# Gathers of an expert layer issued in blocks of eight U rows and eight V rows instead of one U and one V in turn

## What is computed

```
def expert_block(args):
    ht, it, gt = args                    # 128 tokens, their 128 indices, their 128 gates
    ue = jnp.take(u, it, axis=0)
    act = jax.nn.gelu(jnp.einsum('tkd,td->tk', ue, ht), approximate=False)
    ve = jnp.take(v, it, axis=0)
    return jnp.einsum('tk,tkd->td', gt * act, ve)
```

## Time and profile before

| What | us |
|---|---|
| median of three runs | 1722.1 |
| the profiled execution | 1728.55 |
| its span | 1727.2 |
| first gather starts | 974.32 |
| last gather starts | 1711.45 |
| from there to the end of the span | 15.75 |

### The profile page before, as it was taken

The page is one execution under the profiler, slowest core; times in us unless marked ns, Lnnn a source line. Parts: engine busy times, 40 slices in busy tenths (PEclk is TensorE's granted clock), DMA queues, the critical chain, the costliest instruction groups (busy, mean ns, idle before and its releaser), DMA issues.

```text
span 1727.2 us, 19148 instructions
## 1 busy us (share of the span) xinstructions
PE 1498.9 (87%) x7183; PEld 1085.7 (63%) x7183; DVE 1079.7 (63%) x1970; ACT 660.7 (38%) x1102; POOL 547.4 (32%) x608
## 2 busy tenths in 40 slices
PE   7999999998999899999999888997775764867775
PEld 6888897887798788888899764543222321323222
DVE  5766645687654666665657576657745755756644
ACT  5545534785453554553735221312211221211111
POOL 1000001211000000000100356666666766766664
PEclk9999999999999999999999999999997987989888
DMA  8555454333353455574444889999999999999997
GB/s 282 179 187 195 150 183 157 107 134 125 106 189 121 156 190 180 193 193 137 130 138 159 292 299 372 346 370 365 370 381 364 362 370 363 388 366 377 369 377 277
DMA packets 199942, 431.87 MB, mean 250 GB/s; under 512 B 20773, under 2 KB 114090, under 8 KB 199850
## 3 DMA queue, kind: packets, MB, share of 16 engines
q0 software_dynamic: 73728, 268.47, 40.8%
q1 hardware_dynamic: 123312, 159.66, 28.5%
q10 hardware_dynamic: 2810, 2.52, 0.5%
HBM read 429.55 MB, written 1.05 MB: 249 GB/s over the span
## 4 chain that ended last, share of the span: by engine, by line
PE 56%; POOL 12%; issue 11%; DVE 10%; ACT 6%; another core or an unknown queue 3%; DMA 2%; DVEq 1%; ACTq 0%; POOLq 0%
PE ps L431 56%; POOL GS L2701 6%; POOL RAW L2701 4%; DVE WL L1789 3%; ACT WH L1261 2%; POOL AR L2701 1%; DMA RAW<-in_peer_v_dram,AR 1%; DMA RAW<-in_peer_u_dram,AR 1%; DVE XN L1826 1%; DVE GS L2538 1%; POOL LB L2701 1%; DVE H L1831 0%; DVE AR L2054 0%; DVE XX L1845 0%
## 5 line engine op out<-in xcount | busy, mean ns | idle before, releaser
L431 PE MATMUL ps<-XX,WH 128*128 128x256 f32 (+1 forms) x1872 | 467.4, 330 | 10.0 <-DVE XX L1845 5.1
L1789 DVE TENSOR_TENSOR WL<-RAW,WH 128x2048 fp32r<-128x2048 f32 x135 | 309.8, 2295 | 185.8 <-ACT WH L1261 185.5
L431 PE MATMUL ps<-XX,WL 128*128 128x256 f32 x1288 | 364.5, 283 | 0.0
L431 PE MATMUL ps<-GS,AR 128*128 128x512 f32 x526 | 266.2, 644 | 95.6 <-issue 44.0
L431 PEld LDWEIGHTS ps<-XX,WH 128*128 128x128 f32 x1872 | 316.9, 192 | 47.3 <-issue 7.1
L1261 ACT ACTIVATE WH<-RAW 128x2048 fp32r<-128x2048 f32 x129 | 247.3, 1917 | 96.5 <-PE ps L431 96.4
L431 PEld LDWEIGHTS ps<-GS,AR 128*128 128x128 f32 x526 | 105.2, 207 | 245.2 <-issue 176.3
L431 PEld LDWEIGHTS ps<-XX,WL 128*128 128x128 f32 x1288 | 247.0, 192 | 0.7
L2591 POOL TENSOR_TENSOR small<-small 128x1 f32<-128x1 f32 x28 | 15.4, 556 | 679.5 <-DVE small L1821 365.6
L431 PE MATMUL ps<-RAW,AR 128*128 128x512 f32 x348 | 175.1, 633 | 56.3 <-ACT AR L1746 33.0
L2538 DVE CUSTOM_DVE_ANT_0 GS<-GS,ps 128x1024 f32<-128x1024 f32 x135 | 162.9, 1216 | 59.3 <-DMA GS<-in_peer_u_dram,AR 42.4
(11 more groups left out here) (377 smaller groups left out, 1850.9 us busy)
## 6 DMA issues: line engine op xcount, KB each, us to landing
RAW<-in_ffn_w_gu_dram SPq DMA_DIRECT2D x44, 1024.0 KB, 5.1
RAW<-in_w_in_dram SPq DMA_DIRECT2D x39, 1024.0 KB, 5.3
RAW<-in_ffn_w_down_dram SPq DMA_DIRECT2D x22, 1024.0 KB, 5.0
RAW<-in_w_out_dram SPq DMA_DIRECT2D x12, 1024.0 KB, 5.0
RAW<-in_xa_wkv_dram SPq DMA_DIRECT2D x8, 1024.0 KB, 5.8
RAW<-in_xa_wq_dram SPq DMA_DIRECT2D x4, 1024.0 KB, 5.2
RAW<-in_xa_wo_dram SPq DMA_DIRECT2D x4, 1024.0 KB, 4.9
RAW<-in_w_peer_q_dram SPq DMA_DIRECT2D x4, 1024.0 KB, 5.7
```

The costliest lines, as they stand in the source:

```text
L431: return nc.tensor.matmul(out_, lhsT, rhs, start=start, stop=stop, skip_group_check=True)
L1789: nc.vector.tensor_tensor(conv(1, k, kt), v, conv(0, k, kt).bitcast(F32), ALU.subtract).then_inc(S["lo"], 1)
```

## The change

Two places are rewritten, the planner that hands out the spots and GpSimd's loop, so that both follow the same new order: eight U rows b to b + 7, then eight V rows b - 8 to b - 1, for b = 0, 8, 16, up to 256. The number of gathers, of spots and of waits' kinds, and the items of the other engines (in their old order) stay.

```
-    for j in range(256 + LAG):
-        ring.extendleft(sorted((s for s in OPEN if OPEN[s][0] == j), key=...
-        for table, row in (("U", j), ("V", j - LAG)):
+    for b in range(0, 256 + LAG, LAG):
+        for table, row in [("U", b + i) for i in range(LAG)] + [("V", b - LAG + i) for i in range(LAG)]:
             if not 0 <= row < 256:
                 continue
+            if table == "U":
+                ring.extendleft(sorted((s for s in OPEN if OPEN[s][0] == row), key=...
             s = ring[0]
             ring.rotate(-1)
...
-        for what, n in SCHEDULE:
-            if what != "items":
-                continue
-            for j in n:
-                for name, table, row in (("U", A["peer_u_2"][0], j), ("V", A["peer_v_2"][0], j - LAG)):
...
-                if j == LAG - 1:
-                    rstd("peer", 1, rs[:, 1:2], msq[:, 1:2])
+        def gather(name, table, row):
...
+        for b in range(0, 256 + LAG, LAG):
+            if b < 256:
+                for row in range(b, b + LAG):
+                    gather("U", A["peer_u_2"][0], row)
+            if b == 0:
+                rstd("peer", 1, rs[:, 1:2], msq[:, 1:2])
+            if b >= LAG:
+                for row in range(b - LAG, b):
+                    gather("V", A["peer_v_2"][0], row)
+            for j in range(b, b + LAG):
                 if j in FINISH and FINISH[j] == 2:
                     rstd("final", 0, rs[:, 0:1], msq[:, 0:1])
```

More of the change, by code:

```diff
@@ L378, in body @@
     fills, left, ring = [0] * len(spots), {s: OPEN[s][1] for s in OPEN}, collections.deque()
-    for j in range(256 + LAG):
-        ring.extendleft(sorted((s for s in OPEN if OPEN[s][0] == j), key=lambda s: (s < AFTER_OUT, s < AFTER_OUT and OPEN[s][1][1], s), reverse=True))
-        for table, row in (("U", j), ("V", j - LAG)):
+    for b in range(0, 256 + LAG, LAG):
+        for table, row in [("U", b + i) for i in range(LAG)] + [("V", b - LAG + i) for i in range(LAG)]:
             if not 0 <= row < 256:
                 continue
+            if table == "U":
+                ring.extendleft(sorted((s for s in OPEN if OPEN[s][0] == row), key=lambda s: (s < AFTER_OUT, s < AFTER_OUT and OPEN[s][1][1], s), reverse=True))
             s = ring[0]
@@ L2685, in pool_program @@
         nc.gpsimd.tensor_copy(iot, ioti).then_inc(S["iota"], 1)
-        for what, n in SCHEDULE:
-            if what != "items":
-                continue
-            for j in n:
-                for name, table, row in (("U", A["peer_u_2"][0], j), ("V", A["peer_v_2"][0], j - LAG)):
[L2691 to L2702, removed]
-                if j == LAG - 1:
-                    rstd("peer", 1, rs[:, 1:2], msq[:, 1:2])
+        def gather(name, table, row):
+            m = row // 16
+            s, _ = slot[name, row]
+            who, k = slot_free[name, row]
+            if who in pe.named:
+                pool.wait_ge(pe.own, pe.nth(who, k))
+            else:
+                pool.wait_ge(S[who], k)
+            pool.wait_ge(dve.own, dve.nth("idx", m + 2 if row > 7 else 1))
+            nc.gpsimd.indirect_dma_start(spots[s], None, table, bass.IndirectOffsetOnAxis(
+                un[m % 3]["idx"][:, row % 16:row % 16 + 1], 0)).then_inc(S["gather%d" % s], 16)
+        for b in range(0, 256 + LAG, LAG):
[8 more added lines that the diff above has]
+            for j in range(b, b + LAG):
                 if j in FINISH and FINISH[j] == 2:
```

## The result

The changed kernel takes 1739.1 us (median of five executions, 1735.2 to 1753.6) where the kernel before takes 1722.1: 1.0104 times as long, 95% interval 1.0085 to 1.0122. It is slower by 17 us. The forecast was 1711 and had the wrong sign; the time lies inside the range, and what happened is the mechanism of rival 3. The profiled execution took 1753.58 us, 25.0 more than that of before, so it shows the loss larger than the median does.

The account below looks back on a forecast made before the run. Gather issue (643 us) plus waits on TensorE's late counts was taken as the bound, DMA's floor 12 us above issuing. Terms 0.6 - 8 - 4 = -11.4 gave 1717.2 profiled, 1711 median; range 1678 to 1748, forecast's own 1692 to 1718.

Parts of the forecast that it names:

- rival 3: VectorE becomes late in groups with choosing, 15 times: +28 us, up to +57, so 1750, up to 1779; chance 0.34.
- What bounds the kernel: Expert layer: issuing 512 gathers takes 643 us; waits come on top because a full gather stream delays TensorE's count.
- Moving: DMA in the expert layer: one gather lands per 1.28 us, 655 us for 512, a floor 12 us above issuing.
- The start: First gathers: U rows 12 and 13 wait longer for query projections, U row 16 goes at 1018.0; cost +0.6 us.
- Waits on TensorE: GpSimd's gathers needing V rows' spots: 15 waits of 4.9 us instead of 27, 69 us against 76.9; -8 us.
- V rows no longer wait for w: V rows issued 17 gathers behind their group's last dot, not 3; TensorE's wait for w ends; -4 us.
- The tail: After the last gather: V 248 to 255 stay the last eight, landing at the same distance from the end; 0.
- Rival 2: Blocks of V rows make the waits on TensorE nearly vanish: 1665 us (1659 to 1692); chance 0.12.
- The signs: Slow side: waits on VectorE ahead of V gathers, dots back to back long after landing, L2565 waiting for gelu every group.

Follow-up runs that it names:

- kind B: Four of the chips used, on which the kernel before takes 1649.5 us; the changed kernel takes 1653.0 us there.
- half rows: Kernel before, each gather after the first in its spot bringing 512 of 1024 columns: 1719.3 us on kind A, 1634.5 us on kind B.
- kind A: Two of the chips used, and those of the first runs, on which the kernel before takes about 1722 us; the changed kernel takes 1739.1 us.

## Why the prediction was wrong

*What bounds the kernel.* Right as a count: issuing at 1.25 us a gather, and waits on top. On kind B 512 gathers are issued in 650 us, the 643 of the text and 7 of waits. Wrong as a cause: the late counts belong to the kind of chip and not to the bytes of the stream, as the half rows and kind B show. What does hold them on kind A stays open. What is excluded: the bytes of the gathers (halved, 85.3 us of waits instead of 91.3) and the granted clock as such, which was 0.89 in the changed kernel's stage on kind B almost without waits and 0.89 before on kind A with them. Not tested on kind A are the number of gathers and TensorE's own work.

*Moving.* I took a DMA floor of 655 us, 12 above issuing. Kind B shows it: DMA is full for some 660 us, and half rows win 15. Right. The Trainium skill (DMA: Bandwidth & Descriptors, Specifications) has about 358 GB/s as one core's share; 409 stood here for 625 us, so this core, which ran alone, was above that share over a long stretch and not only over 5 us.

*The start, +0.6.* U row 16 starts at 1013.28 and not at 1018.0: the query projections were there earlier (U row 12 at 993.06, row 13 at 999.51, before 997.93 and 1004.20). Beside the 1.0 us that the stage begins later, a gain of 5 where I had a loss of 0.6; it was used up by the 64th gather, which starts 6.6 us later than before.

*Waits on TensorE, -8.* 91.3 fell to 48.1, but not by the term's reasoning: with the choosing left out the blocks have 97.8 us of them and the old order 81.3, so blocks by themselves add some. In the changed kernel GpSimd stands at a dot in that time. The cycle that I guessed, one wait of 4.9 us every 32 gathers, does appear where VectorE is out of the way, with 5.5 us each; that it would save time was wrong.

*V rows no longer wait for w, -4 or up to +57.* Here the prediction failed. It said that the last dot of a choosing group would be done 17 us after landing, within 24, from a group of 27 us; "nearest to the one row that shows such a wait" it took -4. Measured, the group takes 35.7 us, since its gaps are 17.7 us and not about 8, and the dot ends 33 to 34 us after issue, beyond the 28.8. The text itself put the turning point at "7 us of further gaps"; 8.7 more came. I had sized the gaps from the mean over all groups in an order where most escaped them. The rows of before hold the full set too, at the same instructions:

```profile
1427.17 0.18 DVE L2458 CAST AR<-AR 128x32 f32<-128x32 uint32 x1 [4.14 <-issue]
...
1432.77 0.43 DVE L2369 MAX8 AR<-AR 128x8 f32<-128x256 f32 x1 [3.92 <-issue]
1434.17 0.09 DVE L2371 MATCH_VALUE_LOAD AR<-AR 128x8 f32 x1 [0.97 <-issue]
...
1436.97 0.09 DVE L2373 MATCH_VALUE_LOAD AR<-AR 128x8 f32 x1 [2.30 <-issue]
...
1439.77 0.43 DVE L2375 MAX8 AR<-AR 128x8 f32<-128x256 f32 x1 [2.31 <-issue]
1441.17 0.09 DVE L2377 MATCH_VALUE_LOAD AR<-AR 128x8 f32 x1 [0.97 <-issue]
```

Before, 15 us of gaps or more came three times in 13 groups (15.0, 21.4 and 21.8 us); in the changed kernel every settled group has 17 to 19. The worst case was in the trace, and the change made it the rule. That the gaps would grow with the change was in no term.

*The tail, 0.* 5.6 us in the profiled execution, which is 14 us above the median; how much of it the median has isn't known.

*Rival 3* said +28, from 2 to 3 us more waiting at each of 15 groups (which would be 30 to 45). Measured: waits on VectorE of 3.4 to 7.7 us in each of the ten settled groups, 67.1 in all, less 43 of TensorE's, +17 by the median and +25 in the profiled execution. Its second leg, ScalarE's gelu behind `diag`, shows outside the settled groups only: w waits for the gelu 20.5 us at 1069, 23.7 at 1167 and 9.6 at 1703. Rival 2 fell: with the V rows in blocks the waits on TensorE did not nearly vanish (97.8 us without choosing).

*The signs* named beforehand came on the slow side, two of three: waits on VectorE ahead of V gathers, and dots back to back after their rows landed (the dots waited 4.1 us for DMA in the changed kernel, 76.8 before, from 1030 to 1715 us). The third, w behind the gelu in every group, did not.

The range held the result by rival 3's chance of 0.34; the forecast itself, 1692 to 1718, did not.

No version beat the kernel before. Blocks of four, and of two, equal it.

## What to carry to other kernels

Where buffers turn in a ring, ask of each consumer how long after issue its worst group ends, not its mean one, and compare this with the ring's depth in time: here 7 to 29 us of 28.8 before, 33 to 34 after. A change of order can turn the worst group into the rule, and the idle time between the steps may itself change with it. And a wait that disappears in one place is worth nothing until the next one behind it is priced: 43 us of waits on TensorE went, and 67 on VectorE came.

## What the runs showed of the hardware

Chips differ. The same kernel takes 1649.5 us on four chips and 1722 on two, and all of the difference lies in this stage (its last gather starts near 1620 where it is near 1711). On the slower kind small VectorE steps that stand behind one another with a drain between them start on a raster in some groups: 1449.46, 1450.86, 1453.66, 1456.46, 1457.86 are 1.40, 2.80, 2.80 and 1.40 us apart, and so are those of the kernel before from 1432.77 on. In other groups of the same trace there is no gap. On the other kind the same steps follow within 0.1 us on average. Half rows still show such groups (from 1428.10 us 1.40, 2.81 and 2.79 apart), and so does every order run on the slower kind; how many groups have them goes with the order. What makes them is open.
